# Head norms of two attentions: sums of squares by one f32 product or by two rounded products

## The chip, the cores and the metric

One core of a Trainium2 chip runs the whole program in one launch. The metric is the time of one execution on the device, in microseconds. Before the change it is 2480.53 us, the median of 3 runs (2477.56 to 2482.07).

## The reference, cut to what matters

Three transformer layers over 512 tokens of width 1024. The change lies in the attention of the first two. Both normalise each head's queries and keys by the root of the mean of their squares, the first one its outputs as well:

```
rms_norm(x, gain):  x * rsqrt(mean(x*x, axis=-1) + 1e-6) * gain

first attention (8 heads):  q, k = rms_norm of (h @ w_qkv) over 64 channels
   weights = softmax(q k^T / 8 + bias) of one half - lam * that of the other
   o = rms_norm(weights @ v, over 128 channels) * (1 - lam_init);  h += o @ w_o
second attention (16 heads): q_nope, k_nope = rms_norm over 128 channels,
   q_pe = rotary(rms_norm over 64 channels);  k_pe shared by the heads
   softmax((q_nope k_nope^T + q_pe k_pe^T) * scale) @ v;  h += o @ w_o
```

Behind each attention stand a convolutional gated feed-forward and a per-layer embedding; the third layer is not touched.

## The kernel before, in words

Activations lie channels on partitions, tokens along the free axis: a tile is 128 channels by 512 tokens, f32. A projection multiplies three times: weights and activations are each kept as a rounded half (type fp32r, names with `_hi`) and a remainder (`_lo`), and `tile` (L439 to L441) adds hi*hi, hi*lo and lo*hi in a bank of `lin`. Weights come in groups by DMA from SP's queue into a ring of three slots; ACT rounds a group (`before`, `high_half`, L1665), POOL subtracts the rounded half from it (L2076), and PE waits for that.

The engines run in their own order, written out by hand, and meet by semaphores. Two banks of `lin` alternate; `take` on DVE (L1019, in the second attention L1346, L1348 and L1351) empties a bank and frees it.

A norm goes like this. DVE's take writes the raw tile (`a_raw`, `b_raw`). ACT squares it (`squared`, L1788 and L1891; the output's square at L1812). PE multiplies a 128x128 matrix of ones (`ones`, or `ones64` with two blocks of 64) by the squares in f32, so that each partition of the bank `stat` holds the sum over channels (`sums`, L573 and L732; L590 for the output). ACT takes Ln and then Exp of -0.5 times it (`inv_sqrt`, L1709 and L1711), over the squares in place: `a_ri` is `a_sq`, `b_ri` is `b_sq`. DVE multiplies (`normed`, L1232 and L1382; L1247 for the output). There is one bank `stat`: PE's next sum waits until ACT's Ln has read the last.

**First attention** (`a_step`, ten steps, one head each, software-pipelined). In step s the projection of head s (`proj`, steps 0 to 7: q, k and v tiles, lin_(0) to lin_(2)), the scores and softmax of head s-1 (`attn`, steps 1 to 8) and the output norm of head s-2 (`tail`, steps 2 to 9) are interleaved. DVE's order in a step: biased(0), take_(0), the output's norm, the remainders of finished outputs (`out_lows`, L988: two chunks in steps 5 and 6, one in 7 and 8), biased(1), weights_(0), take_(1), biased(2), weights_(1), biased(3), normed(0), weights_(2), weights_(3), normed(1), take_(2), and the copy of the attention's product. `biased` (L1208) adds the bias and takes the maximum, `weights_` (L1218 to L1225) scales by the reciprocal. ACT's: the output's square, exps(0), square of tile 0, the output's factor, exps(1), the next weights' rounding, square of tile 1, exps(2), factor_(0), exps(3), factor_(1), rounding, copies. PE's: scores(0), lin_(0), the output's sum, scores(1), lin_(1), scores(2), sums(0), scores(3), sums(1), lin_(2), turns, product with v. Steps 8 and 9 already multiply and add tiles of the output projection a_wo0 (`early`, on DVE L996). Before step 9 DVE subtracts chunk 6 of the outputs (`before_last`), which waits for ACT's rounding of it (L1674) in step 9.

**Second attention** (`b_step`, ten steps, one pair of heads each; projection in steps 0 to 7, scores and softmax in 1 to 8, the late part with v in 2 to 9). Seven tiles per pair: two q_nope, q_pe, two k_nope (0 to 4, which are normalised) and two of values. DVE: take_(0), biased(0), take_(1), take_(2), output(0), weights_(0), biased(1), normed(0), take_(3), normed(1), output(1), weights_(1), take_(4), biased(2), normed(2), take_(5), normed(3), the rotary terms, weights_(2), biased(3), take_(6), normed(4), weights_(3). ACT: squared(0), exps(0), copies of the last step, squared(1), squared(2), the first rounding of the next weights (`split(0)`, 128x1536), factor_(0), exps(1), squared(3), factor_(1), squared(4), exps(2), factor_(2), turned(0), factor_(3), exps(3), turned(1), factor_(4), the second rounding, turned(2). PE: lin_(0), score(0), turn_(3), lin_(1), product(0), lin_(2), sums(0), score(1), product(1), lin_(3), sums(1), lin_(4), score(2), sums(2), turn_(0), lin_(5), sums(3), the rotation, score(3), turn_(1), lin_(6), sums(4), turn_(2).

## Time and profile before

| what | value |
|---|---|
| median of 3 runs | 2480.53 us |
| the profiled execution | 2478.39 us |
| its span, first to last instruction | 2476.6 us |
| mean granted TensorE clock | 0.963 |
| busy: PE, PE's weight loads | 2323.7 us, 1784.8 us |
| busy: DVE, ACT, POOL | 1197.3 us, 913.4 us, 836.7 us |
| first attention, steps 0 to 9 | some 30 to 303 us of the span |
| second attention, steps 0 to 9 | some 803 to 1157 us |

A row of a timeline is one instruction, or several of a kind: its start and its length in us, engine, line, operation, tiles, shape, and in brackets the time that the engine had stood idle and what released it. Records of PE overlap, so the time a product takes is read from one start to the next. An f32 product leaves two records, a rounded one leaves one. Engine sums in the views by stretch are busy time; the difference to the stretch is time without work. The step boundaries are named here by the instructions around them, since the program does not mark them.

### The profile page before, as it was taken

What the parts mean: (1) busy time and instruction counts of PE and PEld (TensorE: products, weight loads), DVE (VectorE), ACT (ScalarE), POOL (GpSimd) and SP (SyncE); (2) the same over time, 40 slices, a digit from 0 to 9 for tenths busy, and PEclk for the clock granted to TensorE, in tenths of its full rate; (3) what the DMA queues carried; (4) which work ended last, traced back from release to release, by engine and by line L of the source; (5) the groups of instructions that cost most, each with busy time, mean ns of one, the idle gap of its engine ahead of it and who ended that gap; (6) DMA issues with size and microseconds to landing.
All of it is one profiled execution on the core that took longest, in us unless ns stands there. A gap on an engine that the chain in (4) does not pass through costs nothing.

```text
span 2476.6 us, 26005 instructions
## 1 busy us (share of the span) xinstructions
PE 2323.7 (94%) x10172; PEld 1784.8 (72%) x10172; DVE 1197.3 (48%) x2159; ACT 913.4 (37%) x1465; POOL 836.7 (34%) x328
## 2 busy tenths in 40 slices
PE   6999899999999899999999999999879899999997
PEld 4666678887877565557888878778774468888876
DVE  4444575553256565653655542447327553333124
ACT  3455443332233544543334322332217333222232
POOL 2222244444433111113444444344310034444442
PEclk9999999999999999999999999999759789999998
DMA  7111133333222101102332322253210023333222
GB/s 255 51 52 47 52 98 100 96 94 105 93 83 83 54 30 35 39 26 78 95 101 94 98 97 96 85 166 101 74 43 1 1 68 94 101 95 107 94 90 77
DMA packets 58347, 201.03 MB, mean 81 GB/s; under 512 B 6416, under 2 KB 10016, under 8 KB 58224
## 3 DMA queue, kind: packets, MB, share of 16 engines
q1 hardware_dynamic: 55360, 194.94, 24.8%
q10 hardware_dynamic: 2864, 4.40, 0.5%
q8 instruction: 82, 1.34, 0.2%
q14 instruction: 41, 0.34, 0.0%
HBM read 197.19 MB, written 7.38 MB: 83 GB/s over the span
## 4 chain that ended last, share of the span: by engine, by line
PE 81%; DVE 8%; ACT 6%; issue 2%; DMA 2%; SPq 0%; POOL 0%; ACTq 0%; DVEq 0%; PEldq 0%
PE lin L439 22%; PE lin L441 22%; PE lin L440 22%; PE lin L780 2%; DVE arena L1382 1%; PE scores L701 1%; PE obank L723 1%; PE turn L536 1%; ACT arena L1709 1%; PE lin L455 1%; PE obank L621 1%; PE lin L457 1%; PE lin L456 1%; PE scores L705 1%; PE scores L852 1%
## 5 line engine op out<-in xcount | busy, mean ns | idle before, releaser
L2076 POOL TENSOR_TENSOR w_lo<-slots,w_hi 128x1024 fp32r<-128x1024 f32 (+3 forms) x322 | 834.2, 2592 | 1483.6 <-ACT w_hi L1665 1483.3
L1665 ACT ACTIVATE w_hi<-slots 128x1024 fp32r<-128x1024 f32 (+3 forms) x322 | 357.4, 1110 | 705.4 <-DMA slots<-in_w_ffn_in 275.6
L439 PE MATMUL lin<-g_hi,w_hi 128*128 128x512 f32 x1416 | 561.4, 396 | 8.9 <-DVE arena L1114 8.2
L441 PE MATMUL lin<-g_hi,w_lo 128*128 128x512 f32 x1416 | 552.4, 390 | 0.0
L440 PE MATMUL lin<-g_lo,w_hi 128*128 128x512 f32 x1416 | 552.3, 390 | 0.0
L439 PEld LDWEIGHTS lin<-g_hi,w_hi 128*128 128x128 f32 x1416 | 266.6, 188 | 80.0 <-issue 24.3
L440 PEld LDWEIGHTS lin<-g_lo,w_hi 128*128 128x128 f32 x1416 | 266.8, 188 | 58.7 <-issue 3.8
L441 PEld LDWEIGHTS lin<-g_hi,w_lo 128*128 128x128 f32 x1416 | 266.6, 188 | 55.8
L439 PE MATMUL lin<-f_hi,w_hi 128*128 128x512 f32 x528 | 208.7, 395 | 4.0 <-DVE f_lo L1055 4.0
L1011 DVE TENSOR_TENSOR h<-lin,h 128x512 f32<-128x512 f32 x72 | 49.7, 691 | 328.7 <-PE lin L441 321.0
L441 PE MATMUL lin<-f_hi,w_lo 128*128 128x512 f32 x528 | 208.5, 395 | 0.0
L440 PE MATMUL lin<-f_lo,w_hi 128*128 128x512 f32 x528 | 208.4, 395 | 0.0
L439 PEld LDWEIGHTS lin<-f_hi,w_hi 128*128 128x128 f32 x528 | 99.2, 188 | 28.7 <-DVE f_lo L1055 4.9
L1727 ACT ACTIVATE arena<-arena,vec 128x512 f32<-128x512 f32 x88 | 71.9, 817 | 129.9 <-DVE arena L1070 129.7
L441 PEld LDWEIGHTS lin<-f_hi,w_lo 128*128 128x128 f32 x528 | 99.2, 188 | 23.8
L440 PEld LDWEIGHTS lin<-f_lo,w_hi 128*128 128x128 f32 x528 | 99.2, 188 | 23.6
L1073 DVE SCALAR_TENSOR_TENSOR arena<-arena,vec 128x512 f32<-128x512 f32 x88 | 74.5, 847 | 79.1 <-ACT arena L1727 79.1
L1070 DVE TENSOR_TENSOR arena<-lin,r 128x512 f32<-128x512 f32 x88 | 60.8, 691 | 106.7 <-PE lin L441 106.5
L1685 ACT ACTIVATE arena<-h 128x512 f32<-128x512 f32 x72 | 45.2, 628 | 175.8 <-DVE arena L956 139.5
L1382 DVE SCALAR_TENSOR_TENSOR arena<-arena,vec 128x512 f32<-128x512 f32 x40 | 45.2, 1130 | 58.3 <-ACT arena L1711 58.3
L439 PE MATMUL lin<-c_mix_hi,w_hi 128*128 128x512 f32 x176 | 69.8, 396 | 2.8 <-POOL w_lo L2076 2.8
L1076 DVE SCALAR_TENSOR_TENSOR arena<-arena,vec 128x512 f32<-128x512 f32 x88 | 70.2, 798 | 3.1
(387 smaller groups left out, 3539.9 us busy)
## 6 DMA issues: line engine op xcount, KB each, us to landing
slots<-in_w_ffn_in SPq DMA_DIRECT2D x132, 512.0 KB, 3.4
slots<-in_w_ffn_out SPq DMA_DIRECT2D x48, 704.0 KB, 4.0
slots<-in_w_ple SPq DMA_DIRECT2D x24, 640.0 KB, 3.8
slots<-in_w_a_qkv SPq DMA_DIRECT2D x24, 512.0 KB, 3.5
slots<-in_w_c_in SPq DMA_DIRECT2D x23, 512.0 KB, 3.5
slots<-in_w_b_wo SPq DMA_DIRECT2D x16, 512.0 KB, 3.4
slots<-in_w_b_pair SPq DMA_DIRECT2D x8, 768.0 KB, 4.2
slots<-in_w_a_wo SPq DMA_DIRECT2D x16, 256.0 KB, 2.6
```

The lines of the kernel that those rows point to most:

```text
L439: pe.matmul(lin[:, parity, :], hi, x_hi, start=k == 0, stop=False)
L440: pe.matmul(lin[:, parity, :], hi, x_lo, start=False, stop=False)
L441: mm = pe.matmul(lin[:, parity, :], lo, x_hi, start=False, stop=k == len(rhs) - 1)
L780: mm = pe.matmul(lin[:, t % 2, 0:2 * NCMP], w[x][:, c * P:(c + 1) * P].bitcast(F32), c_zp[:, k // 4, 8 * (k % 2) + c, :], start=c == 0 and ...
L1011: ve.tensor_tensor(h[:, 2 * i + k, :], lin[:, (t + j) % 2, :], h[:, 2 * i + k, :], ALU.add)\
L1070: ve.tensor_tensor(f_u[:, k, 2:S + 2], lin[:, (t0 + k) % 2, :], r[:, :], ALU.mult)\
L1073: ve.scalar_tensor_tensor(out=f_c[:, k, :], in0=f_u[:, k, 1:S + 1], scalar=vec[:, w + 1:w + 2], in1=f_c[:, k, :], op0=ALU.mult, op1=ALU.ad ...
L1076: ve.scalar_tensor_tensor(out=f_c[:, k, :], in0=f_u[:, k, 0:S], scalar=vec[:, w:w + 1], in1=f_c[:, k, :], op0=ALU.mult, op1=ALU.add).then_ ...
L1382: ve.scalar_tensor_tensor(out=dst, in0=b_raw[:, j, :], scalar=v1(vname), in1=b_ri[:, j, :], op0=ALU.mult, op1=ALU.mult).then_inc(q.b_norme ...
L1665: ac.activation(w_hi[:, slot, at_], slots[:, slot, at_], ACT.Copy).then_inc(q.hi_made, 1)
L1727: ac.activation(f_c[:, k, :], f_u[:, k, 2:S + 2], ACT.Identity, bias=vec[:, w + 3:w + 4], scale=vec[:, w + 2:w + 3]).then_inc(q.f_first, 1)
L2076: po.tensor_tensor(w_lo[:, slot, at_], slots[:, slot, at_], w_hi[:, slot, at_].bitcast(F32), ALU.subtract).then_inc(q.weights_split, 1)
```

## The change

Each square is made twice on ACT: once written as the rounded type (`a_sq_hi`, `b_sq_hi`), once in f32. DVE then subtracts the first from the second in place (`square_split`, giving `a_sq_lo`, `b_sq_lo`), and PE multiplies ones, rounded as well, by the one and by the other, both into `stat` (`sum_of_squares`). The output's square of the first attention is treated in the same way. The matrices of ones are copied once into a rounded tensor. Three buffers for the second attention's rounded squares lie over `r` and the embedding's input `p_in_t`, so that the load of that input (`load_p(1)`) moves from before to behind this attention. In the first attention, chunk 6 of the outputs is subtracted within step 9 instead of before it. Some semaphores of other stages are merged, with the same waits.

```diff
+            def sum_of_squares(m, hi, lo):
+                pe.matmul(stat[:, :], ones_r[:, m, :], hi, start=True, stop=False)
+                return pe.matmul(stat[:, :], ones_r[:, m, :], lo, start=False, stop=True)
...
@@ PE, first attention @@
-                        pe.wait_ge(q.a_squared, 2 * s + j + 1)
+                        pe.wait_ge(q.a_sq_split, a_splits(s, j))
-                        pe.matmul(stat[:, :], ones64, a_sq[:, j, :], start=True, stop=True).then_inc(q.a_summed, 1)
+                        sum_of_squares(1, a_sq_hi[:, j, :], a_sq_lo[:, j, :]).then_inc(q.a_summed, 1)
-                    pe.wait_ge(q.a_osquared, s - 1)
+                    pe.wait_ge(q.a_sq_split, a_splits(s, 2))
-                    pe.matmul(stat[:, :], ones, a_sq[:, 2, :], start=True, stop=True).then_inc(q.a_osummed, 1)
+                    sum_of_squares(0, a_sq_hi[:, 2, :], a_sq_lo[:, 2, :]).then_inc(q.a_osummed, 1)
@@ PE, second attention @@
-                        pe.wait_ge(q.b_squared, 5 * s + j + 1)
+                        pe.wait_ge(q.b_sq_split, 5 * s + j + 1)
-                        pe.matmul(stat[:, :], ones64 if j == 2 else ones, b_sq[:, j, :], start=True, stop=True)\
-                            .then_inc(q.b_summed, 1)
+                        sum_of_squares(int(j == 2), b_sq_hi[j % 3], b_sq_lo[:, j, :]).then_inc(q.b_summed, 1)
@@ DVE, behind the wait for r_ready @@
+            ve.wait_ge(q.consts_in, 16)
+            ve.tensor_copy(ones_r[:, 0, :], ones)
+            ve.tensor_copy(ones_r[:, 1, :], ones64)
@@ DVE, first attention @@
+                def square_split(j, squared, n):
+                    if n > 0:
+                        ve.wait_ge(squared, n)
+                        ve.tensor_tensor(a_sq_lo[:, j, :], a_sq[:, j, :], a_sq_hi[:, j, :].bitcast(F32), ALU.subtract)\
+                            .then_inc(q.a_sq_split, 1)
                 biased(0)
+                square_split(2, q.a_osquared, 2 * (s - 1) if tail else 0)
                 take_(0)
...
-                if attn and tail:
-                    out_lows(0, a_o, a_o_hi, a_o_lo, {5: (0, 1), 6: (2, 3), 7: (4,), 8: (5,)}.get(s, ()))
+                if tail:
+                    out_lows(0, a_o, a_o_hi, a_o_lo, {5: (0, 1), 6: (2, 3), 7: (4,), 8: (5,), 9: (6,)}.get(s, ()))
                 biased(1)
                 weights_(0)
+                square_split(0, q.a_squared, 4 * s + 2 if proj else 0)
                 take_(1)
...
                 weights_(1)
                 if attn:
                     early(1)
+                square_split(1, q.a_squared, 4 * s + 4 if proj else 0)
                 biased(3)
...
-            a_steps(ve, a_step, lambda: out_lows(0, a_o, a_o_hi, a_o_lo, (AH - 2,)))
+            a_steps(ve, a_step)
@@ DVE, second attention @@
-                take_(0); biased(0); take_(1); take_(2); output(0); weights_(0); biased(1); normed(0); take_(3); normed(1)
-                output(1); weights_(1); take_(4); biased(2); normed(2); take_(5); normed(3)
+                take_(0); biased(0); take_(1); square_split(0); take_(2); output(0); square_split(1); weights_(0); biased(1)
+                square_split(2); normed(0); take_(3); normed(1); output(1); square_split(3); weights_(1); take_(4); biased(2)
+                square_split(4); normed(2); take_(5); normed(3)
@@ ACT, first attention (the output's square likewise) @@
+                        ac.activation(a_sq_hi[:, j, :], a_raw[:, j, :], ACT.Square).then_inc(q.a_squared, 1)
                         ac.activation(a_sq[:, j, :], a_raw[:, j, :], ACT.Square).then_inc(q.a_squared, 1)
@@ ACT, second attention @@
+                        wait(ac, q.b_summed, 5 * s + j - 2)
+                        ac.activation(b_sq_hi[j % 3], b_raw[:, j, :], ACT.Square).then_inc(q.b_squared, 1)
                         ac.activation(b_sq[:, j, :], b_raw[:, j, :], ACT.Square).then_inc(q.b_squared, 1)
...
-            load_p(1)
             factor("attn1")
...
             b_steps(b_step)
+            load_p(1)
             residual_squares("b_wo1", "ffn1")
```

## Rows read from the trace of the kernel before

**Rows 1.** The page, part 4: the chain that ended last, shares by engine.
```profile
PE 81%; DVE 8%; ACT 6%; issue 2%; DMA 2%; SPq 0%; POOL 0%; ACTq 0%; DVEq 0%; PEldq 0%
```

**Rows 2.** Busy time by engine in one step of the second attention; times in us.
```profile
990.00:1027.20 37.20, 34.44 (x153) 22.51 (x153) 22.33 (x49) 18.69 (x41) 5.86 (x2) 1.00 0.12 36
```

**Rows 3.** PE timeline, one step of the second attention: start, length, line, tiles, [idle before <-releaser].
```profile
930.30 1.10 PE L732 MATMUL stat<-arena,consts 128*128 128x512 f32 x2 [0.94 <-ACT arena L1709]
...
938.31 0.79 PE L536 MATMUL turn<-consts,g 128*128 128x128 f32 x4 [1.57 <-ACT low L1913]
```

**Rows 4.** DVE timeline, the same step.
```profile
915.56 0.69 DVE L1346 TENSOR_TENSOR arena<-lin,lnr 128x512 f32<-128x512 f32 x1 [4.25 <-PE lin L441]
916.17 0.68 DVE L1389 COPY arena<-obank 128x512 f32<-128x512 f32 x1
...
919.56 2.83 DVE L1382 SCALAR_TENSOR_TENSOR arena<-arena,vec 128x512 f32<-128x512 f32 x1
922.30 0.69 DVE L1348 COPY arena<-lin 128x512 f32<-128x512 f32 x1
924.93 0.75 DVE L1382 SCALAR_TENSOR_TENSOR arena<-arena,vec 128x512 f32<-128x512 f32 x1 [1.94 <-ACT arena L1711]
```

**Rows 5.** ACT timeline, the same step.
```profile
916.28 0.63 ACT L1891 ACTIVATE arena<-arena 128x512 f32<-128x512 f32 x1 [4.31 <-DVE arena L1346]
916.82 1.47 ACT L1665 ACTIVATE w_hi<-slots 128x1536 fp32r<-128x1536 f32 x1
...
923.03 0.63 ACT L1891 ACTIVATE arena<-arena 128x512 f32<-128x512 f32 x1 [2.30 <-DVE arena L1348]
...
929.49 0.67 ACT L1709 ACTIVATE arena<-stat,eps 128x512 f32<-128x512 f32 x1
```

**Rows 6.** POOL timeline, the same step.
```profile
918.37 3.47 POOL L2076 TENSOR_TENSOR w_lo<-slots,w_hi 128x1536 fp32r<-128x1536 f32 x1 [12.40 <-ACT w_hi L1665]
```

**Rows 7.** Chain in order of time, last step of the second attention: start, us, what.
```profile
1063.98 0.23 PE lin L440
...
1064.44 0.86 PE stat L732 x2
```

**Rows 8.** DVE timeline, steps 4 and 5 of the first attention.
```profile
158.59 0.16 DVE L1220 TENSOR_TENSOR small<-small 128x1 f32<-128x1 f32 x1
...
159.73 0.28 DVE L1208 CUSTOM_DVE_ANT_0 arena<-scores,arena 128x128 f32<-128x128 f32 x1
...
187.08 0.69 DVE L1019 TENSOR_TENSOR arena<-lin,r 128x512 f32<-128x512 f32 x1 [0.32 <-PE lin L441]
...
188.61 0.89 DVE L1220 TENSOR_TENSOR small<-small 128x1 f32<-128x1 f32 x1
...
190.47 0.28 DVE L1208 CUSTOM_DVE_ANT_0 arena<-scores,arena 128x128 f32<-128x128 f32 x1
```

**Rows 9.** Timeline of all engines, step 9 of the first attention.
```profile
297.35 1.36 DVE L988 TENSOR_TENSOR a_o_lo<-arena,a_o_hi 128x512 fp32r<-128x512 f32 x1 [5.38 <-ACT a_o_hi L1674]
...
299.57 0.47 PE L455 MATMUL lin<-a_o_hi,w_hi 128*128 128x512 f32 x1 [1.91 <-DVE h L996]
```

**Rows 10.** PE timeline, steps 4 and 5 of the first attention.
```profile
160.12 1.10 PE L573 MATMUL stat<-arena,consts 128*128 128x512 f32 x2 [0.98 <-ACT arena L1709]
...
190.13 1.10 PE L573 MATMUL stat<-arena,consts 128*128 128x512 f32 x2 [0.98 <-ACT arena L1709]
```

**Rows 11.** POOL timeline, steps 4 and 5 of the first attention.
```profile
155.90 2.38 POOL L2076 TENSOR_TENSOR w_lo<-slots,w_hi 128x1024 fp32r<-128x1024 f32 x1 [6.21 <-ACT w_hi L1665]
...
187.12 2.36 POOL L2076 TENSOR_TENSOR w_lo<-slots,w_hi 128x1024 fp32r<-128x1024 f32 x1 [7.41 <-ACT w_hi L1665]
```

**Rows 12.** Timeline of ACT, step 0 of the first attention.
```profile
51.51 1.06 ACT L1665 ACTIVATE w_hi<-slots 128x1024 fp32r<-128x1024 f32 x1 [13.04 <-DMA slots<-in_w_a_qkv]
```

**Rows 13.** Busy time by stretch as in group 2; after the engines: PEclk, DMA share, GB/s.
```profile
274.40:278.00 3.60, 3.59 (x9) 2.85 (x10) 1.82 (x7) 1.34 (x5) 1.28 (x1) 0.53 0.00 0
817.00:827.00 10.00, 6.12 (x25) 3.57 (x25) 5.67 (x6) 4.41 (x8) 2.73 (x1) 1.00 0.01 2
```

More of the change, by code:

```diff
@@ L135, in wait, with a_splits @@
         eng.wait_ge(sem, value)
+def a_splits(s, j):
+    before = 2 * min(s, AH) + max(0, s - 2)
+    return before + 1 if j == 2 else before + (s >= 2) + j + 1
 def a_steps(eng, step, before_last=None):
@@ L187, in build_program @@
         w_hi = nc.alloc_sbuf_tensor_at("w_hi", [P, RING, SLOT], F32R, offset=top[0]); top[0] += 4 * RING * SLOT
-        r = sb("r", P, S)
+        r, r_hi = sb("r", P, S, rounded="r_hi")
         lnr = sb("lnr", P, S)
@@ L195, in build_program @@
         small = sb("small", P, 64)
-        p_in_t = sb("p_in_t", P, 2, S)
+        p_in_t, p_in_hi = sb("p_in_t", P, 2, S, rounded="p_in_hi")
         arena_at = top[0]
@@ L1811, in a_step @@
                     ac.wait_ge(q.a_otaken, s - 1)
+                    ac.activation(a_sq_hi[:, 2, :], a_rawo, ACT.Square).then_inc(q.a_osquared, 1)
                     ac.activation(a_sq[:, 2, :], a_rawo, ACT.Square).then_inc(q.a_osquared, 1)
@@ L1972, in _ @@
             ac.wait_ge(q.gl_abs, 2)
-            ac.activation(gl_l, gl_l, ACT.Exp, scale=-1.0).then_inc(q.gl_exp, 1)
-            ac.wait_ge(q.gl_exp, 1)
+            ac.activation(gl_l, gl_l, ACT.Exp, scale=-1.0).then_inc(q.gl_abs, 1)
+            ac.wait_ge(q.gl_abs, 3)
             ac.activation(gl_l, gl_l, ACT.Ln, bias=ones[:, 0:1]).then_inc(q.gl_ln, 1)
```

34 lines of the change are left out of this document (21 added, 13 removed).

## The prediction

> **What bounds the kernel now.** I read the page's chain first. It is PE for 81% [rows 1], which would make every microsecond taken from PE a gain. The chain is an average, though, so next comes the step itself: in one steady step of the second attention, 37.2 us, PE is busy 34.4, DVE 22.3, ACT 18.7 and POOL 5.9 [rows 2]. PE has 2.8 us without work, and the question is who ends those pauses. The PE timeline of one such step shows two: 0.94 us before the fourth sum of squares, ended by ACT's L1709 (the Ln that frees the stat bank), and 1.57 us before the turns of L536, ended by ACT's copies [rows 3]. So between the take of the third tile and the last turns it is a relay between DVE and ACT that sets the step, and PE only afterwards, from there to the next step's third tile.
>
> The relay, in DVE's and ACT's rows [rows 4, 5]: take_(2) at 915.56; ACT's square, then the weight rounding L1665, then POOL's 3.47 us of L2076 from 918.37 to 921.84 [rows 6]; DVE's normed(0) is issued at 919.56 and takes 2.83 us where the same line takes 0.75 at 924.93. It ends 0.55 after POOL does: it was held. Behind it come take_(3) at 922.30, square(3) at 923.03, Ln(1), normed(1), output(1), weights_(1), take_(4), square(4), exps(2), Ln(2) at 929.49, and with it PE's fourth sum at 930.30.
>
> **What the change does to PE.** A sum of squares is now one f32 product, two records in 0.86 us of the chain, while a rounded product of the same 128x512 takes 0.23 [rows 7]. Two rounded ones are 0.46, so each sum saves 0.40. There are 64 in the code: 16 for q and k and 8 for the outputs in the first attention, 40 in the second. All on the path would be 25.6 us.
>
> **What it adds, second attention, steps 1 to 7 (heads' projection and attention together).** Each of five squares is issued twice on ACT (0.54 from one ACT start to the next, 916.28 to 916.82 [rows 5]), and each gets a subtraction on DVE (0.61 from one 128x512 start to the next, 915.56 to 916.17 [rows 4]). Not all lie on the relay:
> - Squares 0 and 1 and their splits fall into ACT's and DVE's pauses before take_(2), or under POOL's piece; cover gone, 0.54 and 0.61 each.
> - Square 2 twice: L1665, queued behind it on ACT, starts 0.54 later, and so does POOL: it ends at 922.38. +0.54.
> - square_split(2) stands on DVE ahead of normed(0), and by then POOL is at work. It reads two tensors in SBUF, as L1382 does, so I take it to be held too: both then run one after the other once POOL is done. +0.61 for take_(3).
> - Square 3 twice, with Ln(1) and normed(1) queued behind it: +0.54.
> - square_split(3), ahead of weights_(1) and take_(4): +0.61.
> - Square 4 twice, ahead of exps(2) and Ln(2): +0.54. Its split falls into DVE's wait for the factor.
> - PE's savings of 0.40 come before waits that end later than now, or after the last one: worth nothing here. The last sum stands before the turns that wait 1.57.
>
> Sum 2.84 per step, 19.9 for seven. Step 0 has no attention; there POOL starts after the second split, so one 0.61 drops out: 2.23, less 0.40 for its last sum, which is followed by tiles with no wait: +1.8. **Second attention +21.7.**
>
> The hold of split(2) is the term with a doubt. If it ran beside POOL, normed(0) would still wait for POOL and only +0.54 would reach take_(3): 2.23 per step. Upwards, a second such hold costs 0.73 (L1220 at 0.89 against 0.16 [rows 8]): 3.57. I take 2.84, because the one DVE subtraction of two SBUF tensors that meets POOL in this trace, L988, took 1.36 [rows 9], about twice its usual length. The Trainium skill (SBUF — State Buffer, Who interferes with whom) says why: a VectorE instruction with two SBUF inputs and a GpSimd instruction that reads SBUF exclude each other for the whole instruction, and the one issued second waits. By that rule every split placed inside a w_lo piece is dearer than its own length, and a step costs 2.84; without it 2.23.
>
> **First attention.** Here PE's saving does reach the path once a step: the output's sum (L590) has its operands in time, −0.40. The path then waits at the second sum of a step (0.98 idle at 160.12 [rows 10], ended by ACT's Ln). Twofold squares push that Ln by 0.54; split(1) comes behind weights_(1) on DVE and is a second end.
> - Steps 2 to 4: weights_(1) ends where biased(3) starts, 159.73. All of it comes 0.40 earlier, but POOL's piece (155.90 for 2.38 [rows 11]) ends 0.54 later, 158.82, and holds L1220 (now 158.59, then 158.19) by 0.63. Split 0.69 and 0.06 to PE: 160.71 against 160.12, less 0.40 saved in that sum: +0.2 each.
> - Steps 5 and 6 also have two output remainders on DVE, and take(1) has only 0.32 spare [rows 8]: 0.54 + 0.61 − 0.32 = +0.83. POOL's piece of that step (187.12 for 2.36) ends at 190.02 instead of 189.48, so weights_(1) ends 0.54 after 190.47, PE starts at 191.76 against 190.13 [rows 10], less 0.40: +1.2 each.
> - Step 1 has no output sum: +0.14 by ACT's path, +0.7 if DVE is held; +0.4. Step 7, with one remainder: 0. Step 8: −0.4.
> - Step 9: today DVE waits 5.38 us for the rounding of chunk 6 [rows 9] with the adding of tile 6 queued behind it, and PE stands 1.91 before the first a_wo1 product. The subtraction now comes after both. With L590's saving that is 2.3, less the 0.67 by which POOL still holds it: −1.6.
>
> **First attention +1.4** (bounds −1.8, with no hold and all of step 9's wait gained, and +4.3, with nothing gained there).
>
> **At nothing.** The two copies of ones on DVE (at most 0.61 each) and step 0's squares end well before ACT's 13.04 us wait for weights behind the bias transfers [rows 12]; cover gone, some 2 us. load_p(1) moves from before the second attention to behind it in ACT's queue and takes its 512 KB along: it is needed only in the embedding stage, a whole feed-forward later, and ACT has pauses there; cover gone, one issue. The other semaphore renamings change no wait.
>
> **Sum.** 21.7 + 1.4 = +23.1 on the profiled execution's 2478.39: 2501.5, so 2502. The median of the runs is 2.1 above that execution, inside what a measurement of this kernel can tell from no change (0.2%, 5 us). Bounds: 15.6 + 1.8 − 1.8 gives 2494; 7 × 3.57 + 2.2 + 4.3 gives 2510.
>
> **Rivals.**
> - *PE is the bound and its saving counts everywhere* (other side, faster). For it: 81% of the chain. Then 2478.4 − 25.6 = 2453; it decides if the relay has more slack than PE has pauses, that is if Ln(2) were not what PE waits for at 930.30. Against it: that row, and the same order in every step.  Chance 0.07.
> - *The clock falls in the longer pauses* (slower still). The pause before the fourth sum grows from 0.94 to about 4 us. For it: 3.6 us at a granted clock of 0.53 [rows 13], nearly all at the lower level of 1.2 GHz, stand in step 8 of the first attention, right behind a wait of PE for a w_lo piece. Against: in step 0, with PE busy 6.1 of 10 us, it stayed at 1.00 [rows 13]. One fall loses up to 1.8 us of PE work; where it outlasts the slack before the turns it reaches the path: 7 × 1.8 more, 2514. The Trainium skill (TensorE: Matmul & The Clock Gate, HAM oscillation) describes this very pattern, bursts of products with waits between them falling to half clock each round; by that rule 2514, by the row of step 0 2502. Chance 0.13.
> - *The additions are covered*: no change, 2478. DVE is idle 15 of 37 us and ACT 18. Against: their pauses are waits for each other. Chance 0.05.
> - *The rounded products are no cheaper with these operands*: PE has slack in the second attention, so only the first's 0.40s go: about +3, 2505. Against: L439 to L441 have the same shape and type. Chance 0.03.
>
> **Chances.** Forecast 0.72, on its own 2494 to 2510. Slower by over 0.2%: 0.72 + 0.13 + 0.03 = 0.88; within: 0.05; faster: 0.07. The range takes in the clock case: 2492 to 2516.
>
> **What would show it.** the 40 sums of the second attention as 80 rounded products, 0.23 us apart; the steady step near 40.0 us instead of 37.2, with PE's idle time from 2.8 to about 7.5; before the fourth sum a pause of some 4 us still ended by L1709; take_(3) about 1.15 after its tile is ready; a split(2) of about 3 us. First attention: steps of 30.0 nearly unchanged, the two with two remainders 31.2. Wrong would be: a second-attention step under 38.5 (the relay had slack, or squares overlap), a split beside POOL at 0.69, or a PEclk under 0.9 in those slices.

## The result, and the profile after

The changed kernel takes 2513.27 us (median of 4 runs, 2509.2 to 2514.07) against 2481.3 us before (4 runs beside it, 2477.56 to 2482.55): ratio 1.0128, 95% interval 1.0111 to 1.0146. It is slower, by 32 us. The profiled execution took 2512.85 us, against 2478.39: 34.5 us where the forecast had 23.1.

The page after, part 4, the chain's shares, nearly those of [rows 1]:

```profile
PE 80%; DVE 10%; ACT 5%; issue 2%; DMA 2%; SPq 0%; POOL 0%; ACTq 0%; DVEq 0%; PEldq 0%
```

They don't tell where 34.5 us went. The length of a step does, taken from one occurrence of a fixed instruction to its next. In the first attention this is DVE's copy of obank into a_rawo (L1284 before, L1311 after), in the second DVE's rope addition (L1408 before, L1442 after). Between these marks the two profiled executions differ by (us; the last column is what the forecast had put at that stretch):

| stretch | before | after | difference | forecast |
|---|---|---|---|---|
| start to the first mark, first attention | 82.95 | 83.79 | +0.84 | +0.4 (step 1) |
| steps 2, 3, 4 | 30.02, 30.04, 29.95 | 31.92, 30.17, 32.95 | +5.0 | +0.6 |
| steps 5, 6 | 30.02, 30.02 | 34.15, 34.18 | +8.3 | +2.4 |
| step 7 | 30.04 | 31.82 | +1.8 | 0 |
| step 8 | 28.24 | 26.27 | −2.0 | −0.4 |
| from there to the first addition of a_wo1 | 11.61 | 10.34 | −1.3 | −1.6 |
| feed-forward, down to the second attention's norms (817.46) | 514.57 | 516.84 | +2.3 | 0 |
| from there to the first rope mark | 12.59 | 14.52 | +1.9 | +1.8 |
| seven steps, second attention | 253.92 | 274.71 | +20.8 | +19.9 |
| from there to the first addition of b_wo1 | 80.31 | 77.07 | −3.2 | 0 |
| the rest | | | 0.0 | 0 |

The sum of the second attention came out as forecast, the first attention did not. Both are to be read in the rows. The 2.3 us of the feed-forward are not the change's: the kernel before is the odd one there. The same stretch took 516.2 to 518.5 us in all ten runs of the experiments, 516.6 in the one whose only edit is the place of chunk 6.

**Second attention.** Busy time of one steady step by engine, in the columns of [rows 13]; it stands against [rows 2]:

```profile
1002.92:1043.03 40.11, 34.42 (x152) 23.49 (x152) 26.06 (x55) 21.27 (x46) 5.89 (x2) 0.92 0.10 33
```

DVE has 3.7 us more than in [rows 2], ACT 2.6, PE nothing less although it does less: its clock is 0.92 of full in the mean. Rows of the four engines' timelines of a step in order of time, where [rows 3 to 6] stand before:

```profile
940.03 0.69 DVE L1373 TENSOR_TENSOR arena<-lin,lnr 128x512 f32<-128x512 f32 x1 [3.65 <-PE lin L451]
...
943.35 3.49 POOL L2114 TENSOR_TENSOR w_lo<-slots,w_hi 128x1536 fp32r<-128x1536 f32 x1 [12.65 <-ACT w_hi L1699]
...
943.98 3.42 DVE L1431 TENSOR_TENSOR b_sq_lo<-arena,p_in_hi 128x512 fp32r<-128x512 f32 x1
...
946.18 0.40 PE L552 MATMUL stat<-p_in_hi,ones_r 128*128 128x512 f32 x1
946.41 0.39 PE L553 MATMUL stat<-b_sq_lo,ones_r 128*128 128x512 f32 x1
...
947.32 0.74 DVE L1409 SCALAR_TENSOR_TENSOR arena<-arena,vec 128x512 f32<-128x512 f32 x1
...
947.98 0.68 DVE L1375 COPY arena<-lin 128x512 f32<-128x512 f32 x1
...
956.79 0.66 ACT L1743 ACTIVATE arena<-stat,eps 128x512 f32<-128x512 f32 x1
...
957.60 0.47 PE L552 MATMUL stat<-r_hi,ones_r 128*128 128x512 f32 x1 [4.05 <-ACT arena L1743]
...
958.96 2.07 PE L765 MATMUL obank<-arena,consts 128*128 128x512 f32 x2 [0.61 <-DVE arena L1409]
```

Two rounded products, 0.23 us from one start to the next, replace the f32 one. From take_(2) (L1373, 940.03) to Ln(2) (L1743, 956.79) it is 16.76 us, against 13.93 in [rows 4, 5]: +2.83, forecast +2.84. 1.21 of it stands at take_(3) already: 7.95 behind take_(2), against 6.74. split(2) is held until POOL's piece of L2114 is done (946.84), 3.42 us against its usual 0.69, and normed(0), in turn, is no longer held at all (0.74, against 2.83). The pause before the fourth sum is 4.05 us.

The seven steps are not alike, though: 35.22, 40.09, 40.13, 40.52, 40.11, 40.10 and 38.53 us, against 30.55 and six times 37.23 before. The last grew by 1.30 only. POOL's piece there is a shorter one, of the next projection's weights:

```profile
1103.76 2.40 POOL L2114 TENSOR_TENSOR w_lo<-slots,w_hi 128x1024 fp32r<-128x1024 f32 x1 [12.39 <-ACT w_hi L1699]
```

In the kernel before, DVE stood idle 1.45 us in that step until PE had the fourth tile ready, so square 2 and split(2) found room: take_(3) comes 6.44 behind take_(2) (before 6.74), and only the 1.3 us behind it are left (take_(2) to Ln(2) 15.25, before 13.93).

**First attention.** PE timeline of step 5, around the second head-norm sum; before it stood as in [rows 10], 17.17 us behind the mark with 0.98 idle:

```profile
195.08 0.49 PE L578 MATMUL scores<-arena 64*128 64x128 f32 x4 [0.55 <-DVE small L1226]
197.69 0.79 PE L552 MATMUL stat<-a_sq_hi,ones_r 128*128 128x512 f32 x1 [2.12 <-DVE a_sq_lo L1261]
198.28 0.63 PE L553 MATMUL stat<-a_sq_lo,ones_r 128*128 128x512 f32 x1
198.70 0.63 PE L449 MATMUL lin<-g_hi,w_hi 128*128 128x512 f32 x1
...
203.40 0.57 PE L451 MATMUL lin<-g_hi,w_lo 128*128 128x512 f32 x1
203.80 0.40 PE L449 MATMUL lin<-g_hi,w_hi 128*128 128x512 f32 x1
204.04 0.39 PE L450 MATMUL lin<-g_lo,w_hi 128*128 128x512 f32 x1
```

The sum starts at 197.69, 18.86 behind the mark of 178.83. The forecast's 191.76 is 18.80 behind before's mark of 172.96, so the wait itself came out within 0.1 us. What follows it did not: the products of L449 to L451 start 0.43 us apart up to 203.4 and 0.23 apart from 203.8 on. The granted clock of the same stretches, with a step that had no such stretch (the third row, step 3) and step 5 itself (the last):

```profile
198.00:200.00 2.00, 2.00 (x6) 1.52 (x6) 1.83 (x9) 1.78 (x6) 0.00 (x0) 0.50 0.00 0
...
204.00:206.00 2.00, 2.00 (x10) 1.64 (x9) 0.00 (x0) 0.00 (x0) 0.00 (x0) 1.00 0.00 0
...
115.71:145.88 30.17, 26.21 (x118) 18.49 (x119) 16.15 (x45) 17.05 (x37) 7.52 (x3) 1.00 0.17 53
...
178.83:212.98 34.15, 29.09 (x118) 20.55 (x119) 16.15 (x45) 19.73 (x41) 7.22 (x3) 0.90 0.16 47
```

(The fall itself runs from 196.9 to 203.8 us.) At 0.50 the clock is 1.2 instead of 2.4 GHz. Step 3, at 1.00 throughout, took 30.17 us, where the forecast had 30.2. The steps with a stretch at half clock took 31.8 to 34.2.

### The profile page after: what moved, and what is told of

It reads as the page before. It is cut to its first block, busy times and chain, and to the rows that moved or that the text cites. A ratio compares the mean times of both kernels' runs of the same rounds, so it can differ in the third digit from the quotient of the medians.

```text
span 2511.1 us, 26172 instructions
## 1 busy us (share of the span) xinstructions
PE 2329.4 (93%) x10172; PEld 1806.5 (72%) x10172; DVE 1243.6 (50%) x2225; ACT 946.7 (38%) x1529; POOL 832.5 (33%) x328
## 4 chain that ended last, share of the span: by engine, by line
PE 80%; DVE 10%; ACT 5%; issue 2%; DMA 2%; SPq 0%; POOL 0%; ACTq 0%; DVEq 0%; PEldq 0%
PE lin L449 22%; PE lin L451 22%; PE lin L450 22%; PE lin L794 2%; DVE b_sq_lo L1431 1%; PE turn L546 1%; PE obank L738 1%; PE scores L716 1%; DVE arena L1409 1%; PE lin L465 1%; PE obank L636 1%; PE lin L467 1%; PE lin L466 1%; PE scores L866 1%; ACT arena L1743 1%
## 5 line engine op out<-in xcount | busy, mean ns | idle before, releaser
L2114 POOL TENSOR_TENSOR w_lo<-slots,w_hi 128x1024 fp32r<-128x1024 f32 (+3 forms) x322 | 830.0, 2579 | 1525.3 <-ACT w_hi L1699 1525.1
L449 PE MATMUL lin<-g_hi,w_hi 128*128 128x512 f32 x1416 | 563.1, 398 | 8.4 <-DVE arena L1128 7.8
L451 PE MATMUL lin<-g_hi,w_lo 128*128 128x512 f32 x1416 | 556.8, 393 | 0.0
L449 PEld LDWEIGHTS lin<-g_hi,w_hi 128*128 128x128 f32 x1416 | 270.1, 191 | 79.4 <-issue 21.9
L451 PEld LDWEIGHTS lin<-g_hi,w_lo 128*128 128x128 f32 x1416 | 269.4, 190 | 57.2
L449 PE MATMUL lin<-f_hi,w_hi 128*128 128x512 f32 x528 | 208.7, 395 | 4.0 <-DVE f_lo L1069 4.0
L451 PE MATMUL lin<-f_hi,w_lo 128*128 128x512 f32 x528 | 208.5, 395 | 0.0
L449 PEld LDWEIGHTS lin<-f_hi,w_hi 128*128 128x128 f32 x528 | 99.2, 188 | 28.5 <-DVE f_lo L1069 4.8
L451 PEld LDWEIGHTS lin<-f_hi,w_lo 128*128 128x128 f32 x528 | 99.2, 188 | 23.8
L1087 DVE SCALAR_TENSOR_TENSOR arena<-arena,vec 128x512 f32<-128x512 f32 x88 | 73.6, 837 | 79.0 <-ACT arena L1761 79.0
L449 PE MATMUL lin<-c_mix_hi,w_hi 128*128 128x512 f32 x176 | 70.4, 400 | 3.4 <-POOL w_lo L2114 3.4
L1090 DVE SCALAR_TENSOR_TENSOR arena<-arena,vec 128x512 f32<-128x512 f32 x88 | 70.2, 798 | 3.1
L451 PE MATMUL lin<-c_mix_hi,w_lo 128*128 128x512 f32 x176 | 69.4, 394 | 0.0
```

Of the source, the lines that this page charges most:

```text
L449: pe.matmul(lin[:, parity, :], hi, x_hi, start=k == 0, stop=False)
L451: mm = pe.matmul(lin[:, parity, :], lo, x_hi, start=False, stop=k == len(rhs) - 1)
L1087: ve.scalar_tensor_tensor(out=f_c[:, k, :], in0=f_u[:, k, 1:S + 1], scalar=vec[:, w + 1:w + 2], in1=f_c[:, k, :], op0=ALU.mult, op1=ALU.ad ...
L1090: ve.scalar_tensor_tensor(out=f_c[:, k, :], in0=f_u[:, k, 0:S], scalar=vec[:, w:w + 1], in1=f_c[:, k, :], op0=ALU.mult, op1=ALU.add).then_ ...
L2114: po.tensor_tensor(w_lo[:, slot, at_], slots[:, slot, at_], w_hi[:, slot, at_].bitcast(F32), ALU.subtract).then_inc(q.weights_split, 1)
```

## The experiments

The kernel before ran beside every experiment, with medians of 2478.5 to 2478.8 us; beside the changed kernel it had 2481.3. Gains over the changed kernel are therefore given twice where it matters, between the medians as they stand and each against its own kernel before; the two ways differ by 2.5 us. Where no interval is given, there is one execution and one time.

### The two halves of the change

Second attention as changed, first as before:

```diff
-                        pe.wait_ge(q.a_sq_split, a_splits(s, j))
+                        pe.wait_ge(q.a_squared, 2 * s + j + 1)
-                        sum_of_squares(1, a_sq_hi[:, j, :], a_sq_lo[:, j, :]).then_inc(q.a_summed, 1)
+                        pe.matmul(stat[:, :], ones64, a_sq[:, j, :], start=True, stop=True).then_inc(q.a_summed, 1)
```

(Not shown: likewise the output's sum, the splits, the doubled squares and chunk 6.)

> The first attention is as before, the second as changed. Theory A (a relay of DVE and ACT sets the second attention's step, and three doubled squares and two splits lengthen it by 2.84 us; the first attention's loss is a matter of its own): steps of the second attention 40.1 us, first attention's steps 30.0, and a kernel some 20 to 22 us slower than before, about 2501. Theory B (the clock's falls are what costs, in both): the second attention's steps come out near 40 only where PEclk falls in them, and the sum is less than 15 us. Rival (PE's saving counts): faster than before.

Measured: 2500.09 us (2495.5 to 2504.41) against 2478.53, ratio 1.0079, interval 1.0062 to 1.0096.

First attention as changed, second as before (not shown: likewise the sums and the doubled squares of the second attention):

```diff
-                take_(0); biased(0); take_(1); square_split(0); take_(2); output(0); square_split(1); weights_(0); biased(1)
+                take_(0); biased(0); take_(1); take_(2); output(0); weights_(0); biased(1); normed(0); take_(3); normed(1)
```

> The first attention is as changed, the second as before, with the load of the embedding's input still behind it. Theory A: steps of the first attention 30.2 without a fall of PE's clock and 32 to 34 with one, as in the changed kernel, so the loss is about 12 to 14 us, and with the one of the second attention alone it sums to the whole. Rival (the loss of the first attention is the additions on DVE and ACT, not the clock): the loss is the same whether or not the clock falls in a step. Forecast on record: +1.4 us.

Measured: 2490.81 us (2489.05 to 2494.15), ratio 1.0052, interval 1.0036 to 1.0069. The halves add: 21.56 + 12.28 = 33.84 us, against 32.0 between the medians of the whole change. The second attention's share is the forecast's 21.7; the first's is 12, not 1.4. The trace of this run holds a comparison of its own: its step 2, the same code as in the changed kernel, ran at a granted clock of 1.00 and took 30.54 us, where the changed kernel's had 0.95 and took 31.9. Its steps 4 to 7, at 0.90 to 0.95, took 31.4 to 33.9.

### Second attention: what lies on the relay

Squares twice, the sum still an f32 product, no subtraction; the first attention is as before here and in the next run:

```diff
-                        pe.wait_ge(q.b_sq_split, 5 * s + j + 1)
+                        pe.wait_ge(q.b_squared, 2 * (5 * s + j + 1))
-                        sum_of_squares(int(j == 2), b_sq_hi[j % 3], b_sq_lo[:, j, :]).then_inc(q.b_summed, 1)
+                        pe.matmul(stat[:, :], ones64 if j == 2 else ones, b_sq[:, j, :], start=True, stop=True)\
+                            .then_inc(q.b_summed, 1)
```

> Only in the second attention each square is made twice on ACT, the first copy going unused; PE multiplies in f32, DVE subtracts nothing. The result is as before. Relay theory: squares 2, 3 and 4 lie on the path, 3 x 0.54 = 1.6 us a step, so steps of 38.85 instead of 37.23 and some 13 us in all. Rival (ACT has pauses enough, 18 of 37 us): steps unchanged.

Measured: 2498.92 us, more than expected. One row each of the DVE and ACT timelines, the two ends of the relay:

```profile
924.47 0.69 DVE L1371 TENSOR_TENSOR arena<-lin,lnr 128x512 f32<-128x512 f32 x1 [4.25 <-PE lin L451]
...
939.94 0.67 ACT L1740 ACTIVATE arena<-stat,eps 128x512 f32<-128x512 f32 x1
```

Busy time by engine in the stretch from mark to mark, two steps:

```profile
946.20:985.00 38.80, 34.94 (x145) 22.38 (x143) 22.39 (x49) 21.26 (x46) 5.86 (x2) 0.96 0.11 35
985.00:1024.36 39.36, 36.86 (x164) 24.02 (x161) 22.45 (x49) 21.38 (x46) 5.87 (x2) 0.96 0.11 34
```

From take_(2) to Ln(2) it is 15.47 us, 1.54 more than before: three squares of 0.54, less 0.08. Steps 2 to 6 are 38.8 us, every other one of them 39.4 (why, was not found). PE's starts lie 3.5 us behind before's at 800 us, ahead of this attention, 17.4 at 1160 and 21.1 at the end: 13.9 us of the 20 belong to the second attention, where the forecast's terms give 13. The other 7 came in stretches whose code this edit leaves alone; they are not explained, and with one execution they can't be told from scatter.

Subtractions alone: squares once, the split written to a tile that nothing reads, the sum an f32 product.

```diff
-                        ve.wait_ge(q.b_squared, 2 * (5 * s + j + 1))
-                        ve.tensor_tensor(b_sq_lo[:, j, :], b_sq[:, j, :], b_sq_hi[j % 3].bitcast(F32), ALU.subtract)\
+                        ve.wait_ge(q.b_squared, 5 * s + j + 1)
+                        ve.tensor_tensor(b_sq_hi[j % 3], b_sq[:, j, :], b_raw[:, j, :], ALU.subtract)\
```

> Only in the second attention DVE makes the five subtractions at their places (of the square and the raw tile, into an unused buffer), PE's f32 product waits for each; squares once. The result is as before. Relay theory: splits 2 and 3 lie on the path, 1.22 us a step: steps of 38.45, some 9 us in all; split(2) takes about 3 us, held behind POOL. If a split beside POOL were not held, 37.85.

Measured: 2487.61 us, 9 above before. (In the trace the seven steps grew by 11.1 us. Step 8 of the first attention and the end of the second, both as before in code, were 1.6 and 1.7 shorter, the first at a clock of 1.00 in place of 0.94.) Rows of the DVE and ACT timelines:

```profile
919.01 0.69 DVE L1371 TENSOR_TENSOR arena<-lin,lnr 128x512 f32<-128x512 f32 x1 [3.65 <-PE lin L451]
...
922.96 3.00 DVE L1429 TENSOR_TENSOR p_in_hi<-arena 128x512 fp32r<-128x512 f32 x1
...
934.31 0.67 ACT L1741 ACTIVATE arena<-stat,eps 128x512 f32<-128x512 f32 x1
```

Busy time by engine in the stretch from mark to mark, one step:

```profile
978.96:1017.60 38.64, 34.52 (x143) 21.93 (x141) 25.55 (x54) 18.69 (x41) 5.99 (x2) 0.96 0.10 35
```

Take_(2) to Ln(2) is 15.30 us: +1.37, two subtractions of 0.61 and 0.15. Squares and splits together are 1.54 + 1.37 = 2.91, and with both in place it is 2.83: the two costs add, as the forecast added them. The subtraction is held here too (3.00 us), without a doubled square in front of it.

The one term of the forecast with a doubt was split(2) ahead of take_(3). So it was put behind it:

```diff
-                square_split(2); normed(0); take_(3); normed(1); output(1); square_split(3); weights_(1); take_(4); biased(2)
+                normed(0); take_(3); square_split(2); normed(1); output(1); square_split(3); weights_(1); take_(4); biased(2)
```

> The changed kernel with the third subtraction of a step of the second attention put behind the copy of the fourth projection tile instead of ahead of the normed product before it. Relay theory: that subtraction (0.6 us of VectorE) is the one that stands ahead of the copy on the chain to the fourth sum, so the copy comes 0.6 us sooner, every step goes from 40.1 to 39.5 us, and the whole is 4 to 5 us below the changed kernel. Rival (the hold of VectorE by GpSimd's split, 3.4 us on that subtraction, is caused by where the subtraction stands): then the hold goes too, a step drops by up to 2.8 us and the whole by some 20. Rival 3 (the third sum, which now gets its remainder later, is late next): steps stay at 40.1.

Measured: 2509.98 us (2506.23 to 2511.45), ratio 1.0123, interval 1.0103 to 1.0142. DVE timeline:

```profile
935.15 0.69 DVE L1373 TENSOR_TENSOR arena<-lin,lnr 128x512 f32<-128x512 f32 x1 [3.65 <-PE lin L451]
...
939.67 2.84 DVE L1409 SCALAR_TENSOR_TENSOR arena<-arena,vec 128x512 f32<-128x512 f32 x1 [0.49 <-ACT arena L1745]
942.44 0.68 DVE L1375 COPY arena<-lin 128x512 f32<-128x512 f32 x1
943.04 0.68 DVE L1431 TENSOR_TENSOR b_sq_lo<-arena,p_in_hi 128x512 fp32r<-128x512 f32 x1
```

Busy time by engine in the stretch from mark to mark, one step:

```profile
917.41:956.86 39.45, 34.45 (x152) 23.52 (x152) 25.50 (x54) 21.28 (x46) 5.88 (x2) 0.93 0.10 34
```

The split is 0.68 again and normed(0) is the one held, 2.84 us. Take_(3) comes 7.29 behind take_(2) instead of 7.95, and a step is 39.45 instead of 40.1: the 0.6 us of the expectation. The seven steps together are 270.9 us against 274.7. The medians can't confirm that: 3.3 us below the changed kernel as they stand, 0.8 with each against its own kernel before. The hold lasts as long as POOL's piece (938.48 to 941.97) and passes to whichever of the two instructions stands there; what the new order gains is only the moved instruction's own 0.6 us.

### Is PE the bound?

One rounded square, one rounded product and no subtraction, in both attentions; chunk 6 is where it was before. The remainder of the squares is left out of the norms. (Not shown: the waits, the second squares and the splits.)

```diff
-                pe.matmul(stat[:, :], ones_r[:, m, :], hi, start=True, stop=False)
-                return pe.matmul(stat[:, :], ones_r[:, m, :], lo, start=False, stop=True)
+                return pe.matmul(stat[:, :], ones_r[:, m, :], hi, start=True, stop=True)
```

> One rounded square by ScalarE per sum, one rounded product by TensorE, no subtraction on VectorE, the output's chunk 6 where it was before the change; both attentions. Left out: the remainder of the squares, so each norm rests on squares rounded once. It asks what the cheaper product alone is worth. TensorE-bound theory: each of the 5 sums of a step of the second attention saves 0.8 us on TensorE, so a step drops from 37.2 to some 33 us, and the whole by some 30 us. Relay theory (a step of the second attention is set by the chain matmul, square, sum, logarithm): what leaves the chain is the difference of product lengths between the sum's start and the logarithm where that sum ends last, 0.86 against 0.23, on perhaps one of the sums: a step of 36.6 to 37.2 us, the whole 0 to 5 us below before. In the first attention the product after the third score matmul ends 0.6 us sooner; TensorE waits less long, so its clock stays high and steps stay at 29.5 to 30.0.

Measured: 2482.68 us, 4 above before. (A sum saves 0.63 here, 0.86 against 0.23, not the 0.8 of the expectation.) Three steps (second attention, step 3 of the first attention, where the clock stayed up, step 5 of it, where it fell), first as busy time by engine, then PE's rows behind the pause of that step 5:

```profile
866.34:903.55 37.21, 32.93 (x150) 22.73 (x149) 22.35 (x49) 18.66 (x41) 5.86 (x2) 0.96 0.11 36
114.91:143.62 28.71, 25.42 (x115) 18.02 (x117) 14.07 (x43) 15.50 (x34) 7.46 (x3) 1.00 0.18 55
173.83:204.39 30.56, 27.02 (x115) 19.18 (x115) 14.86 (x41) 18.13 (x38) 7.42 (x3) 0.94 0.17 53
```

The timeline:

```profile
190.59 0.67 PE L552 MATMUL stat<-a_sq_hi,ones_r 128*128 128x512 f32 x1 [1.13 <-ACT arena L1738]
191.05 0.63 PE L449 MATMUL lin<-g_hi,w_hi 128*128 128x512 f32 x1
...
194.78 0.39 PE L450 MATMUL lin<-g_lo,w_hi 128*128 128x512 f32 x1
```

In the second attention PE has 40 cheaper sums and no added work stands against them. Its busy time in a step fell from 34.4 us [rows 2] to 32.9, the lower clock included, and the step is 37.21 as before: the saving is worth nothing there, and the theory of PE as the bound is out. In the first attention the expectation that the clock would stay up was wrong. In step 3 it did, and the step went from 30.0 to 28.71 us. In the other five of steps 2 to 7 it fell, behind a pause of 1.09 to 1.14 us where before had 0.98 [rows 10] and no fall (steps 2 to 7 of before have a granted clock of 1.00), and the step was 30.2 to 30.6 us, longer than before. A shorter product alone turned into a slower step. The pause of step 3 was 1.09 too, so its length alone does not decide.

### The first attention: the wait or the clock?

The changed kernel with six rounded products whose result nothing reads, ahead of the second head-norm sum, where PE waits anyhow:

```diff
                 score(3)
+                if proj and attn:
+                    for _ in range(FILL):
+                        pe.matmul(turn[:, 0, :], ones_r[:, 0, :], g_hi[:, 0, :], start=True, stop=True)
                 sums(1)
```

> The changed kernel with six extra rounded products (their result is never read) on TensorE in the first attention, right ahead of the second head-norm sum, where it now waits 2.1 us for the remainder of the squares. Clock theory (the excess over forecast in the first attention is TensorE running at half clock for 3.4 to 6.8 us behind that wait): the wait shrinks to some 0.7 us, the clock no longer falls behind it, steps go from 32 to 34 us to 30.2 to 31.3, and the whole is 8 to 12 us below the changed kernel, near 2503. Rival (the steps are long because VectorE is late: the splits push its queue back): extra products on TensorE can't help, steps stay at 32 to 34 and the whole at 2513 or slightly above.

Measured: 2502.17 us (2500.8 to 2502.5), ratio 1.0088, interval 1.0068 to 1.0107. By doing more it is 11.1 us below the changed kernel as the medians stand, 8.6 with each against its own kernel before, and 10.5 between the profiled executions; 10.2 of these lie in the first attention. PE timeline of step 5:

```profile
190.89 1.67 PE L617 MATMUL turn<-g_hi,ones_r 128*128 128x512 f32 x6
193.09 0.50 PE L553 MATMUL stat<-a_sq_hi,ones_r 128*128 128x512 f32 x1 [0.54 <-DVE a_sq_lo L1265]
193.43 0.39 PE L554 MATMUL stat<-a_sq_lo,ones_r 128*128 128x512 f32 x1
193.66 0.39 PE L450 MATMUL lin<-g_hi,w_hi 128*128 128x512 f32 x1
193.88 0.40 PE L451 MATMUL lin<-g_lo,w_hi 128*128 128x512 f32 x1
...
195.94 0.39 PE L451 MATMUL lin<-g_lo,w_hi 128*128 128x512 f32 x1
```

Busy time by engine in the stretch from mark to mark, one step:

```profile
174.22:205.56 31.34, 27.85 (x124) 19.54 (x125) 16.17 (x45) 19.63 (x41) 7.52 (x3) 1.00 0.17 51
```

The sum starts at 193.09, 18.87 behind the mark of 174.22. In the changed kernel it was 18.86. DVE ends the wait at the same place in both; only the products behind it differ, here 0.228 apart (ten starts from 193.66 to 195.94). The step is 31.34 us instead of 34.15, and that difference of 2.8 us is what the rows of the changed kernel give: 1.01 from 197.69 to 198.70 against 0.57 from 193.09 to 193.66; 5.10 from 198.70 to 203.80, twelve starts, which at 0.228 would be 2.74. Together 2.8.

Steps 2 to 8 of this run are 30.53, 30.17, 30.09, 31.34, 31.38, 30.28 and 27.85 us, the first six at a granted clock of 1.00. The forecast had 30.2 three times, 31.2 twice, 30.0, and 27.8.

The run says something of the second attention too, whose code is the changed kernel's. Its steps 1 to 3:

```profile
836.42:869.83 33.41, 28.16 (x115) 19.16 (x114) 21.46 (x41) 18.90 (x36) 5.86 (x2) 0.90 0.12 40
869.83:909.93 40.10, 33.67 (x152) 22.98 (x150) 25.99 (x55) 21.28 (x46) 5.88 (x2) 0.96 0.10 34
909.93:950.03 40.10, 34.53 (x154) 23.60 (x152) 26.05 (x55) 21.29 (x46) 5.88 (x2) 0.92 0.10 34
```

A step is 40.10 us at a clock of 0.96 and at 0.92. The first is 33.41, where the changed kernel has 35.22: there the clock is at half from 838.7 to 848.9, up to 1.9 us into the step, here only until 5.2 us ahead of it, and the whole difference is reached 3.5 us into the step.

Both repairs together, this fill and split(2) behind take_(3), their edits as shown above:

> The changed kernel with both repairs: six extra unread products ahead of the second head-norm sum of the first attention, and the third subtraction of a step of the second attention behind the copy of the fourth tile. If the two effects are independent, as the relay theory (second attention) and the clock theory (first) have it, the gains add: 11.1 + 3.3 to 4.5 us below the changed kernel, near 2498; steps of the second attention 39.45, of the first 30.1 to 31.4. What is then left over the kernel before, some 19 us, is the forecast's relay of 7 x 2.2 us and step 0. If the steps of the second attention change through the first's clock (one gate over both), the sum differs by more than 3 us.

Measured: 2499.73 us (2498.5 to 2504.81), ratio 1.0087, interval 1.007 to 1.0104. Steps are 39.43 and 31.36 us. It is 13.5 us below the changed kernel where the two gains add to 14.4, or 11.0 where they add to 9.4 with each against its own kernel before: they are independent within what these runs can tell.

### What of the change is worth keeping

Chunk 6's remainder alone, moved into step 9 of the kernel before:

```diff
-                if attn and tail:
-                    out_lows(0, a_o, a_o_hi, a_o_lo, {5: (0, 1), 6: (2, 3), 7: (4,), 8: (5,)}.get(s, ()))
+                if tail:
+                    out_lows(0, a_o, a_o_hi, a_o_lo, {5: (0, 1), 6: (2, 3), 7: (4,), 8: (5,), 9: (6,)}.get(s, ()))
-            a_steps(ve, a_step, lambda: out_lows(0, a_o, a_o_hi, a_o_lo, (AH - 2,)))
+            a_steps(ve, a_step)
```

> The kernel before with one thing changed: the rounding remainder of the output's chunk 6 of the first attention is computed in step 9, right behind the normed output, instead of ahead of that step's last work. By the forecast this alone takes 1.6 to 2 us off the last step and its end section, and nothing else moves: 2476.5 to 2477 against 2478.5, steps of the second attention 37.2. If it gave no gain, the shorter end of the first attention in the changed kernel came from elsewhere (the rounded product of the output's norm).

Measured: 2478.53 us (10 runs) against 2478.82, ratio 0.9994, interval 0.9982 to 1.0005, so nothing that these runs can tell from no change. In its trace the stretch from the last a_rawo mark (291.20) to the first a_wo1 addition is 10.56 us, against 11.61: the gain is there, 1.05 us, less than the 1.6 to 2 expected. DVE timeline:

```profile
297.62 0.69 DVE L996 TENSOR_TENSOR h<-lin,h 128x512 f32<-128x512 f32 x1 [0.64 <-PE lin L441]
298.23 2.30 DVE L988 TENSOR_TENSOR a_o_lo<-arena,a_o_hi 128x512 fp32r<-128x512 f32 x2
301.76 0.69 DVE L1011 TENSOR_TENSOR h<-lin,h 128x512 f32<-128x512 f32 x1 [1.23 <-PE lin L457]
```

The addition of tile 6 now stands ahead of the two subtractions; before, it stood behind the first ([rows 9], L996).

With chunk 6 in step 9, only the output's sum of the first attention split, the sums of q and k and the second attention as before (against the kernel before; `a_splits` returns s - 1 here; not shown: the output's two squares and its subtraction):

```diff
-                    pe.wait_ge(q.a_osquared, s - 1)
-                    pe.matmul(stat[:, :], ones, a_sq[:, 2, :], start=True, stop=True).then_inc(q.a_osummed, 1)
+                    pe.wait_ge(q.a_sq_split, a_splits(s, 2))
+                    sum_of_squares(0, a_sq_hi[:, 2, :], a_sq_lo[:, 2, :]).then_inc(q.a_osummed, 1)
```

> Of the change only the output's sum of the first attention is split (ScalarE's two squares of the output, VectorE's subtraction ahead of the first take, two rounded products), and chunk 6's remainder stands in step 9; sums of q and k and the whole second attention are as before. By the forecast's terms 0.40 us leaves TensorE's path in each of the eight steps that have this sum, with nothing on the path against it, and step 9 gives the 1.1 us that moving chunk 6 alone gave: steps of 29.6 instead of 30.0 us, together 4 us, near 2475 against 2479. Rival, from the run with one rounded product per sum: a shorter product only lengthens TensorE's next wait (0.98 to 1.4 us), and where its clock then falls a step loses 1.5 us: steps of 29.6 to 31, the whole 2474 to 2482. Rival 2: the wait for ScalarE's logarithm stands later by the doubled output square (0.54 us), steps unchanged: 2477.

Measured: 2475.66 us (11 runs, 2470.95 to 2477.43) against 2478.75, ratio 0.9985, interval 0.9976 to 0.9994. The interval lies below 1: this version beats both kernels, by 3 us. Its trace, of one of its fastest executions, is 7.0 us shorter than before's; 5.2 of these stand where before's clock fell and this one's did not (step 8, and behind the second attention). Its step 5 as busy time by engine, then PE at that step's second head-norm sum:

```profile
171.85:201.46 29.61, 26.88 (x118) 18.49 (x118) 15.46 (x42) 18.58 (x39) 7.41 (x3) 1.00 0.17 54
```

The timeline:

```profile
188.62 1.10 PE L587 MATMUL stat<-arena,consts 128*128 128x512 f32 x2 [0.98 <-ACT arena L1740]
```

The step is 0.41 us shorter, one sum's saving, and the later sum's wait has stayed at 0.98: what ends it moved up along with PE. The clock stayed at 1.00 in this step.

## Why the prediction was right, and where it was wrong

The direction and the range held (2513.27 in 2492 to 2516, slower). The central number is 11 us low, and the median lies beyond the forecast's own 2494 to 2510. The range holds it because it was widened for a rival of 12.6 us that was to come in the second attention; some 11 us came in the first. That part is luck. By its steps:

- **PE's saving, 0.40 per sum, worth nothing in the second attention.** Right: the products are 0.23 apart, and one product alone left the step at 37.21 us. In the first attention the one sum in three that was to count did: 0.41.
- **Second attention, 2.84 per step.** Right for a steady step: 2.83 on the relay, 2.9 in four of the seven steps, and the parts alone 1.54 and 1.37. Wrong for the last step, which has a shorter piece of POOL's: 1.30, so the seven were 1.54 overcounted. The hold of split(2), the term with the doubt, came as taken. The rule of the Trainium skill (SBUF — State Buffer, Who interferes with whom) was weighed there: the trace agrees, the subtraction lasts to just past POOL's end, 3.42 us and 3.00 in two kernels, and 0.68 where it stands outside POOL's piece. Step 0's +1.8 was +1.9, but with the clock at half for part of it; with less of that, in the fill run, it was 1.2.
- **First attention, the wait.** Right: 18.86 us behind the mark, forecast 18.80, and with the clock kept up the steps are the forecast ones within 0.3 us.
- **First attention, the sum of +1.4.** This is the step that failed. It costed the longer pause at its own length and let PE run on at full clock behind it. Measured it is 12.7 us between the profiled executions and 12.3 in the run with the first attention alone; the six unread products take 10.2 of the 12.7 away again and leave +2.5. What was missing is a term of up to 2.8 us in each step where the clock fell.
- **The rival of the falling clock** named the mechanism and looked at the wrong attention. It was weighed by the pause that grew most (0.94 to 4.05 us), in the second. There the clock did fall, in every one of the seven steps (mean 0.89 to 0.94, [rows 2] had 1.00), and cost little: four of them are 40.09 to 40.13 us, where the relay gives 40.07. One is 0.5 over. The first is 1.8 over its forecast, and the fill run shows that this was half clock. That these 2.3 us and the 1.5 overcounted in the last step nearly cancel is why the sum, 20.8 against 19.9, looks better than its parts. Behind the fourth sum of a step stand waits for DVE and ACT anyway (0.61 at 958.96), and PE's slower products fill them. In the first attention the pause grew by only 1.1 us, but behind it stands an unbroken row of projection products, each of which is on the path. The rule cited for that rival (the Trainium skill, TensorE: Matmul & The Clock Gate, HAM oscillation) agrees with the second attention, a pause of 4.05 us and a fall in each step. The falls of the first attention stood behind pauses of 1.7 to 2.4 us, and of 1.1 in the single-product run, shorter than the waits between bursts that the section describes. What a fall costs is decided by what stands behind the pause.
- **Step 9.** −1.6 forecast, −1.3 measured, 1.05 of it by chunk 6 (the run with it alone), the rest by the cheaper output sum. Step 8 gave 2.0 instead of 0.4: before had its clock at half right there ([rows 13], 0.53), after did not. The run with the subtractions alone, whose first attention is that of before, had no fall there and took 26.7 us, 1.6 less than before.
- **After the second attention's last step** nothing was forecast, and 3.2 us came back. PE's clock before and after, in the same place of the last step's work:

```profile
1096.00:1102.00 6.00, 5.67 (x18) 4.53 (x19) 5.96 (x10) 4.07 (x8) 1.85 (x1) 0.72 0.00 0
```

```profile
1133.00:1139.00 6.00, 6.00 (x26) 4.55 (x25) 5.96 (x9) 3.11 (x6) 2.49 (x1) 1.00 0.00 0
```

  The kernel before loses clock there, the changed one does not; in the version with only the output's sum changed, whose second attention is that of before, the clock of that place is 1.00 and the stretch 77.07 us as well; in the fill run, whose second attention is the changed one, the clock fell there and the stretch is 80.26. So this is no gain of the second attention's change but a fall of the clock that the kernel before happened to have.
- **Of the signs named beforehand**, PE's idle time in a step of the second attention is 5.7 us, not 7.5: half-clock products count as busy. The steps of the first attention, which were to stay near 30.0 and 31.2, are the ones that failed: five of steps 2 to 7 took 31.8 to 34.2. A granted clock under 0.9, named as a sign of an error, stood in one step, the first of the second attention (0.89); the steps of the first attention that lost most have 0.90.
- **Rivals.** PE as the bound and the covered additions are refuted by the single-product and the split parts. Products no cheaper: refuted, 0.23.

Left open: why the clock falls in some steps and not in others of the same code. The pause before the second sum was 2.00 us in step 3 of the changed kernel, without a fall, and 1.97 in step 4, with one; in step 2 it was 2.38 with a fall in the changed kernel, and 2.39 without one in the run with the first attention alone. Whether in the single-product run it was the pause, longer by 0.1 us, or the shorter products ahead of it that brought the clock down was not tested.

## What to carry to other kernels

A pause added to TensorE has two prices: its length, and the products behind it at half clock. Look at what follows the pause: where waits follow, the second price is mostly hidden; where an unbroken row of products follows, it was the larger one here (in step 5 the awaited sum starts 1.7 us later behind the mark, and half clock adds 2.8). The dependent chain between VectorE and ScalarE was forecast well here, 2.84 us a step against 2.83, by counting every instruction queued on it, by start-to-start times; multiply such a step only by the steps that are like it; and a sum made cheaper is worth its saving only where no later wait of the same step takes it back: here that was one sum in three of the first attention and none in the second.

## What the hardware showed that was not expected

- Giving TensorE 6 unread products per step made the kernel some 10 us faster (2502.17 against 2513.27 us; 8.6 with each against its own kernel before), without moving the end of the wait in step 5 by more than 0.01 us.
- Shortening a product with nothing added against it lengthened steps of the first attention from 30.0 to 30.2 to 30.6 us, with a wait of 1.09 to 1.14 us in place of 0.98 and half clock behind it.
- VectorE's hold by GpSimd's piece passes from instruction to instruction with the order (3.42 and 0.74, or 2.84 and 0.68): whichever stands beside the piece waits for its end.
